# A convolution by even and odd lags, dealt out inside the product ahead of it, in a two-block transformer kernel

## The reference

```python
h = x * (1.0 + sc1) + sh1
z = h @ w_in[l] + b_in[l]                          # 2048 -> 9216
z_u, z_v, z_h, z_g = jnp.split(z, split_pts, axis=-1)
y_a = spatial_gating(gelu(z_u), gelu(z_v), ...) @ w_branch_a[l]
y_b = hyena(z_h, ...) @ w_branch_b[l]
gate_a, gate_b = jnp.split(jax.nn.sigmoid(z_g), N_BRANCHES, axis=-1)
mix = (gate_a * y_a + gate_b * y_b) @ w_o[l] + b_o[l]
x = layer_norm(DEEPNORM_ALPHA * x + g1 * mix, ln1_g[l], ln1_b[l])
...
def hyena(...):                                    # z: 256 tokens x 3*1024 channels
    v, x1, x2 = jnp.split(short_conv(z), 3, axis=-1)
    y = v
    for n, gate in enumerate((x1, x2)):
        k_spec = two_sided_spectrum(filt[:, 0, n], filt[:, 1, n])
        y = gate * fft_long_conv(y, k_spec, skip[n])   # convolution over 256 lags, by spectra
```

## Time and profile before

| | us |
|---|---|
| median of 3 runs (2532.17 to 2542.75) | 2534.09 |
| the profiled execution, its own time | 2535.02 |
| its span in the trace | 2533.2 |
| PE busy (matmuls) | 2467.1 |
| DVE busy | 1708.3 |
| ACT busy | 1032.3 |
| DMA, mean over the span | 217 GB/s |

### The profile page before, as it was taken

The page is one execution under the profiler, slowest core; times in us unless marked ns, Lnnn a source line. Parts: engine busy times, 40 slices in busy tenths (PEclk is TensorE's granted clock), DMA queues, the critical chain, the costliest instruction groups (busy, mean ns, idle before and its releaser), DMA issues.

```text
span 2533.2 us, 31225 instructions
## 1 busy us (share of the span) xinstructions
PE 2467.1 (97%) x13558; PEld 2101.8 (83%) x13558; DVE 1708.3 (67%) x1613; ACT 1032.3 (41%) x942; POOL 21.0 (1%) x44
## 2 busy tenths in 40 slices
PE   7999999999999999989999999999899999999998
PEld 7988888787778888778888888898788888888886
DVE  7766567776677777766676786657775655555555
ACT  4543454334334334354544342133443343443442
POOL 0000000000000000000000000000000000000000
PEclk9999999999999999999999999999999999999999
DMA  6333466676776887855666774245555555555552
GB/s 256 135 117 133 166 211 260 265 289 252 291 286 255 313 305 288 308 216 214 233 259 256 270 274 170 100 183 183 199 183 187 195 184 195 187 185 198 183 195 105
DMA packets 78634, 549.94 MB, mean 217 GB/s; under 512 B 8763, under 2 KB 10966, under 8 KB 12833
## 3 DMA queue, kind: packets, MB, share of 16 engines
q1 hardware_dynamic: 74832, 528.25, 56.3%
q0 software_dynamic: 3664, 19.69, 2.0%
HBM read 541.61 MB, written 6.29 MB: 216 GB/s over the span
## 4 chain that ended last, share of the span: by engine, by line
PE 85%; DVE 8%; ACT 3%; DMA 2%; issue 1%; SPq 0%; ACTq 0%; DVEq 0%
PE ps L530 25%; PE ps L531 13%; PE ps L543 11%; PE ps L545 10%; PE ps L544 10%; DVE w_lo L1349 3%; DMA stage<-wstream 2%; ACT w_hi L969 2%; PE ps L528 2%; PE ps L498 1%; PE ps L499 1%; PE ps L500 1%; PE ps L918 1%; PE ps L906 1%; PE ps L816 1%
## 5 line engine op out<-in xcount | busy, mean ns | idle before, releaser
L1349 DVE TENSOR_TENSOR w_lo<-stage,w_hi 128x2048 fp32r<-128x2048 f32 x402 | 918.1, 2288 | 533.1 <-ACT w_hi L969 530.5
L969 ACT ACTIVATE w_hi<-stage 128x2048 fp32r<-128x2048 f32 x402 | 766.3, 1910 | 859.1 <-DMA stage<-wstream 396.7
L530 PE MATMUL ps<-xs,w_hi 128*128 128x512 f32 x3000 | 1063.6, 398 | 3.5 <-DVE w_lo L1349 2.5
L531 PE MATMUL ps<-xs,w_lo 128*128 128x256 f32 x3000 | 842.9, 281 | 0.0
L530 PEld LDWEIGHTS ps<-xs,w_hi 128*128 128x128 f32 x3000 | 563.5, 188 | 140.4 <-DVE w_lo L1349 5.2
L531 PEld LDWEIGHTS ps<-xs,w_lo 128*128 128x128 f32 x3000 | 567.5, 189 | 4.1 <-issue 0.2
L543 PE MATMUL ps<-w_hi,hs 128*128 128x512 f32 x1024 | 402.3, 393 | 9.9 <-DVE w_lo L1349 9.9
L544 PE MATMUL ps<-w_hi,hs 128*128 128x512 f32 x1024 | 400.0, 391 | 0.0
L545 PE MATMUL ps<-w_lo,hs 128*128 128x512 f32 x1024 | 399.8, 390 | 0.0
L543 PEld LDWEIGHTS ps<-w_hi,hs 128*128 128x128 f32 x1024 | 192.9, 188 | 54.6 <-DVE w_lo L1349 12.7
L544 PEld LDWEIGHTS ps<-w_hi,hs 128*128 128x128 f32 x1024 | 193.1, 189 | 40.6 <-issue 0.7
(11 more groups left out here) (372 smaller groups left out, 2430.4 us busy)
## 6 DMA issues: line engine op xcount, KB each, us to landing
stage<-wstream SPq DMA_DIRECT2D x497, 1024.0 KB, 4.9
spectra<-k_made POOLq DMA_DIRECT2D x4, 1024.0 KB, 4.2
k_spec<-spectra POOLq DMA_DIRECT2D x4, 1024.0 KB, 6.7
xraw<-xT SPq DMA_DIRECT2D x4, 512.0 KB, 11.1
resid<-x SPq DMA_DIRECT2D x2, 1024.0 KB, 15.2
out<-out_t SPq DMA_DIRECT2D x4, 512.0 KB, 2.6
c_row<-c_row POOLq DMA_DIRECT2D x1, 1024.0 KB, 5.1
w<-w POOLq DMA_DIRECT2D x8, 128.0 KB, 4.3
```

Of the source, the lines that this page charges most:

```text
L530: pe.matmul(o2, hi, rhs[:, k, :], start=(first and j == 0), stop=False)
L531: mm = pe.matmul(o2[:, S:2 * S], lo, rhs[:, k, 0:S], start=False, stop=False)
L969: act.activation(w_hi[:, w % HIGH, 0:m], stage[:, n % RING, 0:m], ACT.Copy).then_inc(hi_ready, 1)
L1349: tt(w_lo[:, slot, 0:m], stage[:, slot, 0:m], f(w_hi[:, w % HIGH, 0:m]), ALU.subtract).then_inc(lo_ready, 1)
```

## The change

1. **Spectra at half the frequencies.** A spectrum of 256 frequencies over 256 lags is made of two products of 128 frequencies each over the even and the odd lags (tokens `j:S:2`): four matmuls of 512 columns in place of eight, then the sum and the difference of the two. So it is done for the filters (`filter_work`) and for the input (`input_spectrum`); the way back makes sum and difference first (`even_odd`) and then takes sixteen matmuls of 128 columns in place of 256. New on DVE are the sums and differences (`join`, `even_odd`, and two operations in each filter part); on ACT the copy of the odd product alone (`take_odd`; for the filters half of the copy that stood there).
2. **Dealt out.** The z_h units move ahead of the gate b units (units 16 to 27 of `T_Z`), and each step of the convolution has a tile number of its own, `T_Z + 37` to `T_Z + 73`, in the tables below. `multiply` becomes `real_part` and `imag_part`, with six operations of 1024 columns in place of four of 1024 and four of 512. `T_BB` runs tile by tile like the others.
3. **Residual parked.** `resid` (2 MB) is stored to DRAM at the start of `T_Z` by POOL and comes back after the last `back`; `k_spec` (one buffer now) and `v_spec` take its place.
4. **`w_ada` earlier.** 20, 20, 20 and 18 tiles in the quarters of `T_MLP1`, and 18 in the first 36 steps of `T_Z`.
5. **Front.** The bias chunks stand at tiles 1, 2, 4, 5, 6, 7 in place of 1 to 6, the first chunk's steps ahead of the split of tile 2, the angles at tile 8 in place of 7. ACT loads its table for the square root and takes the first root at tile 17 in place of 18; DVE makes `r_kv` behind the evacuation of tile 19 in place of ahead of it; one `rope` moves by one tile, as do those of `q_rope`; ACT's copy for `swa_hi` moves to tile 21. Two semaphores (`mod_cleared` into `ones_ready`, the two of the transforms into one) are joined.

```diff
+TURN_AT = {37: 0, 47: 1, 57: 2, 62: 3}
+TAKE_AT = {38: 0, 48: 1, 58: 2, 64: 3}
+SPECTRUM_AT = {38: 0, 49: 1, 59: 2, 66: 3}
+JOIN_AT = {40: 0, 50: 1, 60: 2, 67: 3}
+REAL_AT = {42: 0, 52: 1, 61: 2, 68: 3}
+IMAG_AT = {44: 0, 54: 1, 62: 2, 69: 3}
+PARTS_AT = {46: 0, 56: 1, 63: 2, 70: 3}
+BACK_AT = {46: 0, 57: 1, 64: 2, 71: 3}
+SKIP_AT = {48: 0, 58: 1, 65: 2, 72: 3}
+GATE_AT = {50: 0, 59: 1, 66: 2, 73: 3}
+CHUNK = {1: 0, 2: 1, 4: 2, 5: 3, 6: 4, 7: 5}
...
-            due = 72 + min(24, max(0, step - T_Z - 3) * 2 // 5)
+            due = 78 + min(18, max(0, step - T_Z - 3) * 9 // 16)
         elif l < UPT:
-            due = 18 * q + (9 if q == 3 else 7) * (l + 1) // 16
+            due = 20 * q + (9 if q == 3 else 8) * (l + 1) // 16
...
-            due = 18 * q + 7 + 11 * (l - UPT + 1) // 16
+            due = 20 * q + 8 + 12 * (l - UPT + 1) // 16
...
-                            mm = pe.matmul(ps[:, 4 + 2 * d + j, :], hid[:, j * P:j * P + P], w3[:, d, :], start=True,
-                                           stop=True)
+                            mm = pe.matmul(ps[:, 4 + 2 * d + j, :], hid[:, j:S:2], w3[:, d, :], start=True, stop=True)
...
+                    link(tt(k_made[:, 0:4:2], ps[:, 4:8:2, :], k_made[:, 1:4:2], ALU.add))
+                    tt(k_made[:, 1:4:2], ps[:, 4:8:2, :], k_made[:, 1:4:2], ALU.subtract).then_inc(
+                        sem("spectrum_taken"), 1)
...
+        pool.wait_ge(sem("f_turned"), 4)
+        pool.dma_start(parked, resid[:]).then_inc(sem("resid_parked"), 16)
...
+        pool.wait_ge(sem("conv_made"), 4)
+        pool.dma_start(resid[:], parked).then_inc(sem("resid_back"), 16)
...
+        def input_spectrum(i):
+            pe.wait_ge(sem("transforms_loaded"), 32)
+            pe.wait_ge(sem("u_ready"), i + 1)
+            if i:
+                pe.wait_ge(sem("conv_added"), i)
+            for m in range(2):
+                for j in range(2):
+                    mm = pe.matmul(ps[:, 4 + 2 * m + j, :], dft_in[:, j, m * P:m * P + P], u_tok[:, j, :], start=True,
+                                   stop=True)
+            mm.then_inc(sem("u_spectrum"), 1)
+
+        def back(i):
+
+            pe.wait_ge(sem("y_made"), i + 1)
+            for c in range(4):
+                for j in range(2):
+                    for m in range(2):
+                        mm = pe.matmul(conv_bank(c)[:, j * P:j * P + P], v_spec[:, 2 * j + m, c * P:c * P + P],
+                                       idft[:, m, j * P:j * P + P], start=(m == 0), stop=(m == 1))
+            mm.then_inc(sem("conv_made"), 1)
...
+        def even_odd(i):
+
+            tt(v_spec[:, 0:2], y_spec[:, 0:4:2], y_spec[:, 1:4:2], ALU.add)
+            tt(v_spec[:, 2:4], y_spec[:, 0:4:2], y_spec[:, 1:4:2], ALU.subtract).then_inc(sem("y_made"), 1)
+            dve.wait_ge(sem("y_made"), i + 1)
...
+                ins = stt(zc, zc, col("skip", 8 * n + k), conv_bank(c).rearrange("p (j q) -> p q j", j=2), ALU.mult,
+                          ALU.add)
```

More of the change, by code:

```diff
@@ L941, in _ @@
-        for w in range(T_BB + 2, T_WO):
+            at_tile = w - T_Z
+            if at_tile in BACK_AT:
+                back(BACK_AT[at_tile])
+            if at_tile in SPECTRUM_AT:
+                input_spectrum(SPECTRUM_AT[at_tile])
+            if at_tile in TURN_AT:
+                turn_input(TURN_AT[at_tile])
+        for w in range(T_BA, T_BB):
+            tile(w, y_a)
+        pe.wait_ge(sem("yb_split"), 2)
+        for w in range(T_BB, T_WO):
             tile(w, y_b)
@@ L1085, in _ @@
                 act.activation(st[:, 22:26], st[:, 18:22], ACT.Exp).then_inc(sem("sink_exp"), 1)
+            if w == T_KR - 1:
+                act.activation(warm[:], ones[:, 0:2], ACT.Sqrt)
+                root()
             if 1 <= b <= NPAIR:
@@ L1240, in _ @@
                 before = job(w - 1)[1]
[L1241 removed]
+                if not U_Z + 16 <= before < U_Z + 28:
                     take_z(before)
+            if w - T_Z in TAKE_AT:
+                take_input(TAKE_AT[w - T_Z])
+            if w - T_Z - 1 in SPECTRUM_AT:
+                take_odd(SPECTRUM_AT[w - T_Z - 1])
             if w == T_Z + 12:
@@ new lines, in skip_add @@
+        def skip_add(i):
+            n, half = divmod(i, 2)
+            dve.wait_ge(sem("conv_made"), i + 1)
+            for c in range(4):
+                k = 4 * half + c
+                zc = z_h[:, k, :].rearrange("p (q j) -> p q j", j=2)
+                ins = stt(zc, zc, col("skip", 8 * n + k), conv_bank(c).rearrange("p (j q) -> p q j", j=2), ALU.mult,
+                          ALU.add)
+            ins.then_inc(sem("conv_added"), 1)
+            dve.wait_ge(sem("conv_added"), i + 1)
@@ new lines, in gate, with conv_work @@
+        def gate(i):
+            n, half = divmod(i, 2)
+            dve.wait_ge(evac_done, U_Z + 22 + 4 * n + 2 * half)
+            zc = z_h[:, 4 * half:4 * half + 4, :]
+            x = z_h[:, 8 * (n + 1) + 4 * half:8 * (n + 1) + 4 * half + 4, :]
+            tt(zc, zc, x, ALU.mult).then_inc(sem("conv_out"), 1)
+        def conv_work(a):
+            if a in JOIN_AT:
+                join(JOIN_AT[a])
+            if a in REAL_AT:
+                real_part(REAL_AT[a])
+            if a in IMAG_AT:
+                imag_part(IMAG_AT[a])
+            if a in PARTS_AT:
+                even_odd(PARTS_AT[a])
+            if a in SKIP_AT:
+                skip_add(SKIP_AT[a])
+            if a in GATE_AT:
+                gate(GATE_AT[a])
@@ L1865, in _ @@
             took_done(tt(mixacc[:, c:c + 2, :], mixacc[:, c:c + 2, :], one_bank(u), ALU.mult), u)
-            if l in (2, 4, 6):
-                gate(l // 2 - 1)
-        yb_lo(0)
-        split(T_BB + 2)
-        gate(3)
-        yb_lo(1)
+            conv_work(w - T_Z)
+            if l in (3, 5):
+                yb_lo(l // 2 - 1)
         def spread(c0):
```

264 lines of the change are left out of this document (111 added, 153 removed).

## The result

The changed kernel takes **2508.7 us** (median of 4 runs, 2507.3 to 2512.0) against 2534.3 beside it: a ratio of 0.989, 95% interval 0.988 to 0.991. The profiled execution took 2509.4 (span 2507.6, before 2533.2).

What follows compares the result with a forecast made beforehand. PE was taken as the bound (85% of the chain). Dealing -35.4, its waits +6.1, gating and denser w_ada +2.5, T_MLP1 -8.7, front -7.5: -43.0 from 2535.0 gives 2492, as median 2491; range 2477 to 2509.

Steps and rivals of the forecast that it cites:

- rival B: T_MLP1: the stream bounds the stage, six moved loads cost 3.4 us each, 20.5 in all; 2507 us, chance 0.17.
- thin margins: Ways back 1 to 3 in T_Z: parts ready by only 1.2 to 1.5 us; 3 us in the range's upper end.
- A: Whole kernel: no new waits, PE never waits at tile 46, stream carries 337 GB/s; 2478 us, chance 0.17.
- the front: Tiles 0 to 41: reordered early steps shorten waits and half clock, -7.5 us in sum.
- C: Convolution on PE: the conversion to half frequencies doesn't pay, +13.4 and up to 10 more; 2510 us, chance 0.04.
- The dealing: Convolution steps spread over T_Z: PE's share -35.4 us, new waits with half clock +6.1.
- the parking: resid stored at the start of T_Z and loaded back later: covered, no cost; some 7 us if it hit the stream.
- the gating piece: T_Z + 14, tile 187: a w_ada tile on DVE ahead of its chain, +2.0 us, other tiles +0.5.
- The gain of 1 at `T_WO`: Start of T_WO: DMAs of the bias rows no longer meet the stream, 1 us gained.
- the step that failed: T_MLP1: -13.7 us from the filters' spectra, +5 for short waits behind w_lo, sum -8.7.
- (a): Front, first tiles: chunk 0 ahead of split 2, shorter v_swa wait and 1 us of L714's, -2.2 us.
- (b): Front, first root at tile 17 and q_nope: the 5.1 us wait falls to 1.6, half clock goes, -6.0 us.

Runs made afterwards that it cites:

- the even deal: The changed kernel with the 20 w_ada tiles of each of T_MLP1's first three quarters dealt 10 and 10 to its halves, not 8 and 12: 2494.5 us.
- the two joined kernels: Changed kernel with w_ada 10/10, first way back at 47, angles in iteration 7, no w_ada at T_Z+14: 2487.4 us; also 9/11 in the first quarter: 2482.9.

## Why the prediction was partly right

**The range: in part luck.** The time stands 0.3 us inside it, for its upper end was rival B's 2507 and some thin margins, and the runs bear out neither as I had them. Some sums were loose as well: B and the 3 us of margins make 2510, A with the front at its best 2475.5, C up to 2514. And the waits of PE came to 61 us with the one at the start and 48 without it, not to 45. None of this moves the forecast of 2491.

**The dealing: right.** PE's pieces have the lengths forecast (3.43, 3.43, 3.57). The one wait at the way back of the first part was put at 4.4 and is 4.24 between two instructions of PE; the half clock behind it was put at 1.7 and is 1.7. The other three ways back wait for nothing, the parking shows nowhere, the gating piece cost 2.5 with its neighbours (2.0 and 0.5 forecast). Terms inside were off, and cancel: `rows` takes 3.56 in both kernels (tile 255 lasts 9.32, its neighbours 5.76), where I had 1.8 from no row, so that the convolution's share of the old stage was 64 and not 66; and `T_Z` grew by 34.9, where I had 36.6. That the sum of these stages came within 0.2 is luck to that extent. The gain of 1 at `T_WO` did not come: the wait of 1.1 on its third tile is in both kernels, and one of 1.4 on its first is new. From the last `T_Z` tile to L558 on `mixs` it is 100.5, not 94 to 95: 3.6 of that is the last way back, which I had booked ahead of the line, and most of the rest are `rows` (1.8) and the wait of 1.4.

`skip_add` with its new reading of PSUM, in the groups of DVE between 1240 and 1573 (count, then busy and mean ns, idle before):

```profile
L1824 DVE SCALAR_TENSOR_TENSOR z_h<-z_h,cols,ps 128x256 f32<-128x256 f32 x12 | 5.0, 475 | 0.0
```

475 ns, against 477 on whole rows. The trace agrees with the row, and not with a penalty by the Trainium skill's page "SBUF — State Buffer", section "Door 1: The DMA port swizzle", were it carried over to VectorE.

**`T_MLP1`: the step that failed.** The stream's account in the dense halves was mis-sized: I took "**+5**: five or six more short waits behind `w_lo`", between ends of 0 and 13.7. Measured is +15 (1.3 against -13.7), beyond the high end. Three things stand behind it. I let the count of the kernel before calm me ("the same count gives 5.2 per half", and PE idled for 1 in the third quarter), and did not ask what its pauses of 6.9 us did for the other halves: the slack behind them was 7.7 to 10.2 us, and the change, which halves the pauses, leaves 3.5 to 7.0. I left out the stores, 1 MB each, in the stream's account. And I priced an edit by where its instructions stand on PE and DVE, not by when its DMA leaves: the sum and difference on DVE moved the store by more than a tile, onto a pair of loads.

The kernel with the products issued twice divides the 15: 8.6 are the loads moved in, the stores and DVE's operations, with the pauses as before, and 6.3 are what halving the pauses took back of the 13.7, each to within the 3 us that executions differ by. How the 8.6 divide further is not settled, for the parts don't add: the late store alone cost 8.9 in the kernel before, the six loads 9.6 in the changed one, and the even deal gives back 14.1. The third quarter, which has no spectrum, lost 2.3 in its tok half (88.5 to 90.8), so density costs something without any pause.

Over a whole half it was not the rate of the DMA that ran out. The windows above show its engines busy for 0.75 and 0.73 of the first two tok halves, at 284 and 283 GB/s; they are full only in stretches, as beside the first store (0.96 at 335 GB/s over 504.2 to 514.6). A load is issued only when its slot is free, that is when the tile in it has been done; what more slots than five would do, no run shows.

The Trainium skill, page "DMA: Bandwidth & Descriptors", section "Bandwidth", gives 341 GB/s for 1 MB. As a rate that a stage can count on it is not borne out here: no half of `T_MLP1` in any kernel moved more than 316, and those that asked 337 and waited moved 278 to 316.

**The front: two terms off.** (a) -2.1 at tile 8 against -2.2, and (b) -6.3 between tiles 10 and 25 against -6.0, were right. One reading in (b) was not: of the 6.8 us at 0.50 PE still waited in the first 1.75, to 177.45, so that 2.5 were lost and not 3.4. The first softmax cost +3.1 where I had +0.7: the wait grew by 1.6, and half clock came behind it, which I had not priced at all there. And half clock came at the head scores, without a wait: +3.2. Taken together the front is 5.5 short, all of it in the clock and one wait.

**Rival B** ("The stream bounds T_MLP1", 2507, 0.17) names the time that was measured within 2 us, and the right stage, but its price (3.4 us per load, 20.5) is not what the runs show: 1.6 us per tile by the kernel with 18 a quarter, and 0.9 for all six where they stand evenly (-12.8 of the -13.7 came).

## What to carry to other kernels

A pause of the busiest engine is income for the stream. Before shortening it, read the slack behind it, and count the loads *and stores* between it and the next pause; if they ask for more than the stream gave in its densest stretch, the gain may be lost, as here, until the loads are dealt anew. Moving six loads by a few tiles was worth as much here as all the arithmetic saved in that stage, and it was worth nothing in the kernel before, so such a table is worth trying anew after each change to the work around it.

## What the runs showed of the hardware

A store of 1 MB from POOL's queue that left together with a pair of the stream's loads made the second of these take 10.4 us (10.44, 10.43, 10.42, and 10.33 in the kernel before with its store held back), and the stores took 9.4 themselves in place of 4.2. The Trainium skill, page "DMA: Bandwidth & Descriptors", section "Issuing engines are not separate DMA queues", says that transfers issued by different engines run on the same DMA engines and interleave; the trace agrees, and gives the price: a second load, which takes 7.0 without a store, took 3.4 more.

The granted clock fell to 0.5 (1.2 GHz) in places where nothing differs that the profile shows. Behind the same wait of 2.7 at L679 it is 0.72 over 88 to 94 us in the changed kernel and 1.00 with the even deal, which has changed nothing up to there:

```profile
88.00:94.00 6.00, 5.27 (x32) 5.27 (x33) 5.31 (x10) 4.36 (x12) 0.00 (x0) 0.72 0.19 81
```

```profile
88.00:94.00 6.00, 5.25 (x44) 5.26 (x45) 5.31 (x10) 4.34 (x12) 0.00 (x0) 1.00 0.23 97
```

At the head scores it fell without any wait in all nine executions whose tile 25 ended between 209.3 and 212.6 us, and in none of the five that ended it from 213.5 on, the same instructions in both sets; the two joined kernels both came there at 210.0, and lost 3.2 and 1.6. What decides it, the traces do not show; the time alone does not. A half clock behind a wait of 2 to 3 us is a chance and not a term of a sum, and each such place is worth 1.5 to 3.2 us here. That is why one profile does not settle an edit of 3 us, and why its stage has to be read.
